# Moving one VectorE step behind a combination in the feed-forward's first token group

## What is computed

```
x = x + W_down( silu(causal_dwconv3(h2 W_gate)) * (h2 W_up) ),  h2 = RMSNorm(x)
D_MODEL = 1024, D_FF = 2816, CONV_W = 3, all float32

g, u = jnp.split(h2 @ w_ffn_in, 2, axis=-1)
gp = jnp.concatenate([conv_buf.astype(g.dtype), g], axis=1)
gc = conv_b + gp[:, 0:T] * conv_w[0] + gp[:, 1:T + 1] * conv_w[1] + gp[:, 2:T + 2] * conv_w[2]
x = x + (jax.nn.silu(gc) * u) @ w_down
```

## Time and profile before

| | before |
|---|---|
| median of 3 runs | 2344.47 us (2340.36 to 2347.28) |
| profiled execution | 2344.27 us |
| its span, first to last instruction | 2342.6 us |
| TensorE (PE) matmuls busy | 2279.5 us, 97% |
| VectorE (DVE) busy | 1545.8 us, 66% |
| POOL busy | 921.4 us, 39% |
| ScalarE (ACT) busy | 852.0 us, 36% |
| mean granted TensorE clock | 0.993 |

### The profile page before, as it was taken

One profiled execution on the slowest core, in us unless ns is written; L12 is line 12 of the kernel. 1 busy time (PEld: TensorE's weight loads), 2 busy tenths in 40 slices (PEclk: granted clock), 3 DMA queues, 4 the chain that ended last, 5 costly groups with the idle time before them and its releaser, 6 DMA issues.

```text
span 2342.6 us, 34616 instructions
## 1 busy us (share of the span) xinstructions
PE 2279.5 (97%) x13687; PEld 2017.3 (86%) x13687; DVE 1545.8 (66%) x2404; ACT 852.0 (36%) x1457; POOL 921.4 (39%) x724
## 2 busy tenths in 40 slices
PE   6999999999999998999999999999999999999999
PEld 5889868888777887888888899999998999999997
DVE  5666656655673446777777867666768776667665
ACT  4555621222232324443343533233334333333331
POOL 4333302222120437454545454445435343444351
PEclk9999989999999999999999999999999999999999
DMA  7433222211154555222222622212224422221221
GB/s 274 163 127 114 88 60 104 82 69 63 50 187 140 189 180 185 90 91 76 87 90 87 237 85 73 71 60 68 73 72 161 168 72 73 72 68 59 73 72 73
DMA packets 152955, 247.43 MB, mean 106 GB/s; under 512 B 18523, under 2 KB 114551, under 8 KB 150727
## 3 DMA queue, kind: packets, MB, share of 16 engines
q1 hardware_dynamic: 152763, 245.16, 30.8%
q0 software_dynamic: 32, 0.07, 0.0%
HBM read 189.28 MB, written 56.87 MB: 105 GB/s over the span
## 4 chain that ended last, share of the span: by engine, by line
PE 73%; DVE 5%; POOL 3%; DMA 2%; issue 2%; ACT 0%; SPq 0%; POOLq 0%; DVEq 0%; ACTq 0%
PE bank L114 13%; PE bank L115 12%; PE bank L116 12%; PE bank L2687 11%; PE bank L2688 11%; PE bank L2689 11%; DMA late_b_raw<-in_w_ffn_in_dram 2%; DVE late_t L3007 1%; DVE late_a_lo L2959 1%; DVE late_acc L3021 1%; POOL late_t_raw L3171 1%; PE bank L1629 1%; PE bank L1633 1%; PE bank L2630 1%; PE bank L2639 1%
## 5 line engine op out<-in xcount | busy, mean ns | idle before, releaser
L2995 DVE TENSOR_TENSOR late_gp<-bank,late_gp 128x384 f32<-128x384 f32 (+1 forms) x330 | 172.3, 522 | 326.9 <-PE bank L2689 326.8
L2687 PE MATMUL bank<-late_a_hi,late_b_hi 128*128 128x384 f32 (+1 forms) x1056 | 343.0, 325 | 6.5 <-DVE late_b_lo L2967 4.9
L2688 PE MATMUL bank<-late_a_lo,late_b_hi 128*128 128x384 f32 (+1 forms) x1056 | 341.8, 324 | 0.0
L2689 PE MATMUL bank<-late_a_hi,late_b_lo 128*128 128x384 f32 (+1 forms) x1056 | 340.7, 323 | 0.0
L3185 POOL TENSOR_TENSOR late_t<-late_t,late_gp 128x768 f32<-128x768 f32 (+1 forms) x66 | 132.4, 2024 | 513.4 <-DVE late_gp L2995 513.4
L114 PE MATMUL bank<-late_d_hi,late_act_hi 128*128 128x512 f32 (+1 forms) x724 | 283.6, 392 | 8.0 <-DVE late_acc L3021 6.2
L116 PE MATMUL bank<-late_d_hi,late_act_lo 128*128 128x512 f32 (+1 forms) x724 | 282.1, 390 | 0.0
L115 PE MATMUL bank<-late_d_lo,late_act_hi 128*128 128x512 f32 (+1 forms) x724 | 282.1, 390 | 0.0
L2687 PE MATMUL bank<-late_a_hi,late_t_hi 128*128 128x384 f32 (+1 forms) x792 | 259.9, 328 | 12.5 <-DVE late_gp L2995 9.9
L3021 DVE TENSOR_TENSOR late_acc<-bank,late_acc 128x512 f32<-128x512 f32 (+1 forms) x374 | 242.6, 680 | 34.1 <-PE bank L116 33.4
L2688 PE MATMUL bank<-late_a_lo,late_t_hi 128*128 128x384 f32 (+1 forms) x792 | 256.2, 323 | 0.0
(11 more groups left out here) (358 smaller groups left out, 5027.3 us busy)
## 6 DMA issues: line engine op xcount, KB each, us to landing
late_b_raw<-in_w_ffn_in_dram SPq DMA_DIRECT2D x66, 1024.0 KB, 5.1
late_d_raw<-in_w_down_dram SPq DMA_DIRECT2D x32, 1024.0 KB, 4.9
att_next_hh<-h_parts SPq DMA_DIRECT2D x16, 1024.0 KB, 4.8
late_a_raw<-h_parts SPq DMA_DIRECT2D x14, 768.0 KB, 5.9
att_x<-in_x_prompt_dram SPq DMA_DIRECT2D x16, 512.0 KB, 5.0
h_parts<-att_h_hi SPq DMA_DIRECT2D x16, 512.0 KB, 3.3
h_parts<-att_h_lo SPq DMA_DIRECT2D x16, 512.0 KB, 4.6
late_x<-in_x_prompt_dram SPq DMA_DIRECT2D x16, 512.0 KB, 3.7
```

Source lines behind the costliest of these rows:

```text
L2687: nc.tensor.matmul(out, w_h, hi[:, c, :], start=first, stop=False, skip_group_check=True)
L2688: nc.tensor.matmul(out, w_h, lo[:, c, :], start=False, stop=False, skip_group_check=True)
L2689: ins_ = nc.tensor.matmul(out, w_l, hi[:, c, :], start=False, stop=last, skip_group_check=True)
L2995: nc.vector.tensor_tensor(dst, bk, src, ALU.add).then_inc(c_dve, 1)
```

## The change

In the first token group (`G.sample`) and in the steps that have a step before them in the group (not `turned`, so steps 1 to 10), the lo part of the first half of the down weights is made behind the first combination of the step. Before, it was made between the two activation differences. In groups 1 and 2 nothing changes.

```diff
             if p is not None:
                 split_act(p, 0)
-                if not turned:
+                if not turned and not G.sample:
                     split_d(p, 0)
                 split_act(p, 1)
             combine(r, 0, 0)
+            if p is not None and not turned and G.sample:
+                split_d(p, 0)
             if turned:
                 split_a(G, S1)
             elif p is not None:
                 split_d(p, 1)
```

## The result

| | before | changed |
|---|---|---|
| median | 2347.08 us (6 runs, 2340.36 to 2347.68) | 2358.08 us (6 runs, 2352.94 to 2361.77) |
| ratio | 1 | 1.0045, 95% interval 1.0033 to 1.0057 |
| profiled execution, its span | 2344.27, 2342.6 us | 2352.94, 2351.2 us |

The changed kernel is slower, by 11 us by the medians; the forecast was no change that can be measured, at 2347.2 us, in a range of 2343.0 to 2354.0.

What follows compares the result with a forecast made beforehand. TensorE was taken as busy nearly throughout, only its idle places winnable. Steps 2 and 3 add 1.7 us, one double wait 1.04, the rest 0: +2.7 on 2344.27, plus 0.2 to the median, gives 2347.2 us; range 2343.0 to 2354.0.

Steps and rivals of the forecast that it cites:

- The first chain: VectorE's second activation difference and first combination ahead of TensorE's fourth product: 0.71 us gap closes, 7.3 us taken alone.
- The sixth product's gap: TensorE waits for the second combination, delayed by splits and POOL's first sum alternating: new gap of 0.37 us per step.
- The second chain: Up weights' load, POOL's four sums, VectorE's taps and additions: unmoved from the step's start, 6.46 us against 6.42 before.
- The zero for steps 4 to 10: TensorE's gain ahead of the addition is given back as a longer gap there: 0 us, against a possible 2.4.
- Steps 2 and 3: POOL's gate sums now ask before the short last tap, so both steps take 37.75 us: 1.7 us more together.
- Step 1: First changed step of group 0: gap shrinks but both splits meet POOL's sums; 0 us, bounds 1.3 either side.
- The double wait: POOL asks before VectorE's long last tap, so long and short tap each wait for a sum: one step, 1.04 us.
- the upper bound of the gain: Ahead of TensorE's seventh product: whole 0.71 us per step kept if POOL's load lands behind both splits.
- Rival B: POOL's gate sums precede the long tap in six to nine steps: 2352.4 to 2355.6 us; chance 0.14.
- The shift: TensorE's seventh product, and the gate weights' load issued behind it, come 0.34 us earlier in the step.
- Its base: Starting time of the whole kernel before: profiled execution of 2344.27 us, taken as 0.2 us below the median.
- Rival C: Plain reading: the 0.71 us gaps ahead of the fourth product vanish, nothing replaces them; 7.3 us less, 2337.2; chance 0.06.

Runs made afterwards that it cites:

- c_after: Changed kernel repeated without any further change, as a second profiled execution: 2359.39 us, ratio to the kernel before 1.0064 (1.0047 to 1.0081).

## Why the prediction was wrong

**The first chain: right.** The second activation difference started behind ScalarE, the gap of 0.71 us closed, and both splits followed the combination. In step 2 of after, VectorE's two splits stand in one row, POOL's first sum between them, and TensorE's sixth product behind:

```profile
972.68 3.45 DVE L2972 TENSOR_TENSOR late_d_lo<-late_d_raw,late_d_hi 128x1024 fp32r<-128x1024 f32 x2
976.06 1.01 DVE L2995 TENSOR_TENSOR late_gp<-bank,late_gp 128x288 f32<-128x288 f32 x2
...
973.60 1.44 POOL L3173 TENSOR_TENSOR late_t_raw<-late_b_raw 128x512 f32<-128x512 f32 x1 [1.14 <-DMA late_b_raw<-in_w_ffn_in_dram]
```

The pair took 3.45 us; the prediction had 965.80 to 969.28, 3.48 us. The sixth product's gap was forecast at 0.37 us and came at 0.29 to 0.33.

**The second chain: right.** The additions kept their place from the start of the step, the 0.3 to 0.4 us won ahead of them went into a longer gap (0.8 for 0.5 us), and steps of 37.67 us took the place of 37.75. The zero for steps 4 to 10 holds for the steps with one wait.

**Steps 2 and 3: right in mechanism.** The tap waits that they lacked came in step 3 of all five profiles and in step 2 of three. However, the baseline of before was one draw: of the first nine steps its copies have such waits in steps 2 and 4 to 6 in one, and in steps 1, 2, 4 to 7 and 9 in the other. So the change moves a share of waits (20 of 30 steps to 46 of 50), not two steps.

**Step 1: missed.** I took 0. It gained a tap wait in all five profiles (37.6 us; before has 36.8, 37.0 and, with such a wait, 37.75), in c_after a double one.

**The double wait: the step that failed.** The prediction counts one such step at 1.04 us. The number was about right (4 in five executions), and that it fell on step 5 in the first profile was luck: none of the other four profiles has one there. Its price was wrong: 2.7 us, since TensorE's clock fell to 1.2 GHz for 3.4 us behind the gap. In step 10, for which the prediction had taken 0, a wait of three taps costs 3.5 us (44.6 for 41.1) in three of five. Its condition, up weights that land later than the splits begin, stands in the prediction only as the upper bound of the gain (0.71 us); that a larger gain ahead of the seventh product sets the gate load off earlier still was not followed up. Rival B is what happened, in weaker form: it named the mechanism and the direction, its condition (seventh product earlier than the room) was met in a few steps and not in most, and at 1.04 us a piece it could not be costly with few. The shift itself was rightly sized (0.34 us; the load came 0.38 us earlier). With the five profiles the terms are 4 double waits of 2.7 us and 3 triple ones of 3.5 us over five executions, 4.3 us per execution, and by difference the other 1.3 us of group 0's 5.6 come from single waits; the prediction had 1.0 and 1.7. That is 5.6 us for its 2.7, and with it alone the time would still lie within the range. Its base was 2.6 us low as well: before has 2347.08 us by six runs, 2344.47 by the three it had. The rest of the measured 11 us is the later start of step 1, where the prediction had no change, and what no trace shows; the cause of both stays open, as said above.

Rival C's mark, step lengths below 36.5 us, was not reached even by the best kernel (36.6). One reading of the earlier trace rows was also off: of its 8 waits for an addition only 7 lie in group 0 (steps 4 to 10); the longest, 1.6 us, stands in the first step of group 1. No term rests on it.

## What to carry to other kernels

An instruction moved off the critical path can set a transfer off earlier, and the transfer releases an engine into work it had just missed; before counting the gain, follow every release that comes earlier to what will run beside it, and look for races of a tenth of a microsecond there. Where two engines take turns on SBUF, it pays to order them by a wait: holding POOL back until the taps were done took 0.2% off the kernel before (ratio 0.9976), while the moved split alone made it slower. And a longer gap on TensorE has to be priced with the clock behind it, not by its length alone.

## What the runs showed of the hardware

- VectorE instructions with two SBUF inputs, the taps among them, and POOL's sums exclude each other for whole instructions and alternate when both have more to do: long tap 0.75 to 1.77 or 1.86 us, short tap 0.28 to 1.28 us. The Trainium skill ("SBUF — State Buffer", Who interferes with whom) has the exclusion and that issue order decides; these rows agree, and they add the taking of turns: a waiting POOL got in between two VectorE instructions that stood back to back, and the other way round. Near a tie the recorded starts don't tell who goes first: POOL's sum went ahead of the long tap with a start up to 0.03 us behind it, and after it from 0.05 us on.
- In group 0 of the changed kernel TensorE's granted clock fell to 1.2 GHz for 3.4 us behind each of the four gaps of 1.9 us and the three of 3.6 to 3.7 us, and behind its gaps of 0.3 to 0.9 us it did not, nor behind the 1.3 us in step 1 of before. In the double waits it made a 1.1 us longer gap cost 2.7 us. It is no certainty: a gap of 2.5 us just ahead of step 1 in c_after (at 926.1 us) and one of 3.4 us in step 10 of the kernel with both splits moved further had no such stretch behind them.
- The stretch ahead of any changed instruction differed by up to 7 us between profiled executions (926.4 to 933.6 us), by 5.5 us between executions of the kernel before; stretches at 1.2 GHz ahead of it (23.9 to 34.1 us) went with most of that. Two single profiles must be compared by stretch, never by their ends.
